# Five reorderings at the ends of three stages, and the decay product one slot earlier, in a two-block fp32 kernel on one core

## The chip, the cores and the metric

The kernel runs on one NeuronCore of a Trainium2 chip, in one launch. The metric is the device time of one execution in microseconds (us). The five engines are named as in the profile: PE is TensorE, DVE is VectorE, ACT is ScalarE, POOL is GpSimd, SP is SyncE. They run their own instruction streams in order and meet only at semaphores.

## The reference

One sequence of 512 tokens, 1024 channels, passes two layers of a first block and one layer of a second. The first layer is a state-space mixer (SSD): a normed input is projected, convolved and gated, and 32 heads in 8 groups run a chunked scan in both directions. Cut to its core, per chunk of 128 tokens:

```python
cum = jnp.cumsum(lac, axis=1)
decay = jnp.exp(jnp.where(causal, cum[:, :, None] - cum[:, None], -jnp.inf))
cb = jnp.einsum('blgn,bsgn->blsg', cc, bc)
y = jnp.einsum('blsgr,bsgrp->blgrp', cb[..., None] * decay, xdt)
y = y + jnp.einsum('blgn,bgrpn->blgrp', cc, state) * jnp.exp(cum)[..., None]
```

The two directions and a skip term are added, the sum is gated by silu(z), normed within its group and multiplied by an output matrix into the residual. The second layer is gated linear attention (GLA) with the same outer form. The second block projects its normed input for a convolution branch and a latent attention with rotary positions, merges them, adds a cross attention and an MLP. All is float32.

## The kernel before, in words

Every large product is streamed. A unit is a 128-row weight block of up to 1024 columns; SP loads it (`load_unit`, line 119), ACT rounds it to its high part (`split_hi`, line 129, instruction on line 137), DVE subtracts to get the low part (`split_lo`, line 140, instruction on line 147), and PE multiplies it in three products per 128 channels (`mm3`, lines 79 to 81) inside `stream_products` (line 159). That function waits for the low part and for a free one of three PSUM banks, and skips a unit that was already streamed (`if n < c.streamed: return`, with a counter kept while the program is built). SP may load unit n only when unit n-2 is split, so a late `split_lo` is a late load; other loads of SP stand in the same queue.

The SSD stage (`ssd_stage`, line 317) is written out by hand as rounds i = 0 to 9 of 8 slots k. In round i, the units of group i are projected (slots 2 and 3: x; 5 and 6: B and C), while the scan of group g = i-1 is computed and the gate z and the norm of earlier groups are finished. From round 3 on, slots 4 and 7 hold the products with the output matrix (`SSD_OUT`, line 288); in rounds 1 and 2 slots 4 and 7 have no unit at all, in round 8 slots 3, 4, 6 and 7. "Round (i, k)" below is round i, slot k. Each engine walks the same slots. What matters here:

- ACT, per slot: the centre tap of the convolution of the unit before (line 870), z (882), `split_hi`, exponentials (895), copies of x (902), the decay's differences for the next groups (929, 935), which wait for rows that SP loads (line 648), and in slot 7 silu of x, B, C and z between two table loads (940 to 947).
- POOL builds cb times dt for four token tiles (lines 736, 740), adds differences (713), and finishes y (703, 707).
- DVE, per slot: the other four taps of the convolution (line 995), `close` for output tiles (adds a PSUM bank to the residual h and frees it, line 963), `split_lo`, the masked cb (1043), x times decay weights (1054), in slots 2 to 5 the decay matrix m(0) to m(3) (line 1073, two buffers), the states (1082, 1087, 1090), and `assemble(g, p)` (977, 980), which turns the sums of head pair p into y: pair 0 as the last thing in slot 7, pair 1 in slot 0 of the next round, behind that slot's `split_lo`.
- PE, per slot: the unit's product; in slot 0 transposes of x and B and the product of B and C (lines 831, 834, 839), which wait for the silu and for both `assemble` of the group before (`s_asm`, 6 g); `contributions` to the states in slots 2 to 4 (773); `y_intra(g, t)` (757), the product of m(t) and x, in slots 3 to 6, after that slot's unit; `y_inter` (788) in slot 6 three times, six products each, and once in slot 7, where it reuses a PSUM bank that `assemble(g, 0)` must have read:

```python
if (p, d) == (1, 1):
    pe.wait_ge(s_asm, 6 * g + 2)
```

In the last rounds of SSD and GLA, `scale_tile` (ACT, line 243) writes the high part of the next stage's input, `scale_rest` (DVE, line 249) its low part, `square_tile` (ACT, 203 and 205) its squares, of which GLA needs two kinds per tile, and `add_squares` (POOL, 217 and 220) sums them; PE multiplies the sums by ones (258; after GLA 1327 and 1328, behind DVE's line 1609).

`mix_project_stage` (line 1691) has 14 units in slots k = 0 to 13. In slot 6 DVE splits unit 8, then multiplies the unit of the rotary key by a sine (lines 1856 to 1866); PE waits in slot 7 for that (line 1763), behind unit 7. In slot 7 DVE refines a norm (lines 184 to 190, 1848), subtracts (1853) and copies the bank of unit 6 (1876).

Of the kernel before, what the change touches and what calls it, by code (L numbers as in the profile page):

```python
# [27 lines left out]
SG = 8  # L28
# [288 lines left out]
def ssd_stage(nc, c, A, plan, gain):  # L317
# [8 lines left out]
    with ExitStack() as ctx:  # L326
# [421 lines left out]
        def _(pe):  # L748
# [42 lines left out]
            for i, k in slots:  # L791
# [27 lines left out]
                if g not in G:  # L819
                    continue  # L820
                if k == 0:
                    pe.wait_ge(s_silu, g + 1)
                    if g == 0:
                        pe.wait_ge(s_v, 17)
                        pe.wait_ge(s_a, 5)
                    if g:
                        pe.wait_ge(s_asm, 6 * g)
                    for t in range(NT):
                        for j in range(2):
                            a = (t % 2) * GW + j * P  # L830
                            pe.transpose(q[t // 2][:, a:a + P], xt[:, g % 2, j, t * P:(t + 1) * P],
                                         c.ident[:, :])
                    for t in range(NT):
                        last = pe.transpose(q[2][:, t * P:(t + 1) * P], bct[:, 0, t * P:(t + 1) * P],
                                            c.ident[:, :])
                    last.then_inc(s_tx, 1)
                    for t in range(NT):
                        b = slice(t * P, (t + 1) * P)
                        last = pe.matmul(q[3][:, b], bct[:, 0, b], cmat(g)[:, b], start=True, stop=True)
                    last.then_inc(s_cb, 1)  # L840
                if 2 <= k <= 4:
                    contributions(g, k - 2)
                if 3 <= k <= 6:
                    y_intra(g, k - 3)
                if k == 6:
                    for d in range(2):
                        y_inter(g, 0, d)
# [103 lines left out]
        def _(dve):  # L951
# [32 lines left out]
            for i, k in slots:  # L984
                g, f = i - 1, i - 2
                pi, pk = before(i, k)
                if pi in G and pk in CONV:
                    cj = CONV[pk]
                    t, ct = tile_of(pi, pk), conv_tile(pi, cj)
                    dve.wait_ge(s_center, 4 * pi + cj + 1)  # L990
                    dst, src = conv_out(pi, cj), bank(c, t)
                    for tp, last in ((0, 0), (1, 0), (3, 0), (4, 1)):
                        o = tp - 2
                        a, b = max(0, -o), T - max(0, o)
                        ins = dve.scalar_tensor_tensor(out=dst[:, a:b], in0=src[:, a + o:b + o],  # L995
                                                       scalar=tap(tp, ct), in1=dst[:, a:b], op0=ALU.mult,
                                                       op1=ALU.add)
                        if last:
                            ins.then_inc(c.bank_free[t % SB], 1)
                        else:  # L1000
                            ins.then_inc(s_tap, 1)
                            taps[0] += 1
                            dve.wait_ge(s_tap, taps[0])
# [12 lines left out]
                if (pi, pk) in SSD_OUT:  # L1016
                    of, half = SSD_OUT[pi, pk]
                    for j in range(1, 4):
                        close(pi, pk, j)
                        if of == SG - 1:  # L1020
                            scale_rest(c, dve, nx, half * 4 + j - 1)
                    if of == SG - 1:
                        scale_rest(c, dve, nx, half * 4 + 3)
                if (i, k) == (NI - 1, 0):
                    assemble(f, 1)
                if unit_in(i, k) is not None:
# [49 lines left out]
                if 3 <= k <= 5 and g in G:  # L1076
# [6 lines left out]
                    else:  # L1083
                        dve.wait_ge(s_st, 7 * g + 3 * j - 2)
                        for d, t in ((0, j), (1, NT - 1 - j)):
# [3 lines left out]
                        dve.wait_ge(s_st, 7 * g + 3 * j)  # L1089
                        dve.tensor_tensor(st[:, j, :], st[:, j, :], q[2 + j % 2][:, :], ALU.add)\  # L1090
                           .then_inc(s_st, 1)
                if k == 7 and g in G:
                    assemble(g, 0)
            next_fine(c, dve, nx)

# [34 lines left out]
def gla_stage(nc, c, A, plan, gain, gains):  # L1130
# [10 lines left out]
    with ExitStack() as ctx:  # L1141
# [190 lines left out]
        def _(act):  # L1332
# [15 lines left out]
            for i, k in slots:  # L1348
# [4 lines left out]
                if GLA_OUT.get((pi, pk), (0,))[0] == GH - 1:  # L1353
                    _, m0, tiles = GLA_OUT[pi, pk]
                    for m in range(m0, m0 + tiles):
                        final = free_value(c, out_tile(GH - 1, m))
                        scale_tile(c, act, nx, m, final)
                        square_tile(c, act, m, final)
                        square_tile(c, act, m, final, gain)
                if k == 0 and f in G:  # L1360
# [330 lines left out]
def mix_project_stage(nc, c, A, cqh, cql, ckh, ckl, tbl, ks, z):  # L1691
# [3 lines left out]
    with ExitStack() as pre:  # L1695
# [107 lines left out]
        def _(dve):  # L1803
# [4 lines left out]
            for k in range(N + 1):  # L1808
                t = tile(k - 1) if k else None
                if 1 <= k <= 5:  # L1810
                    dve.wait_ge(c.tile_done, t + 1)
                    dve.tensor_tensor(lat[:, k - 1, :], bank(c, t)[:, :], c.rstd, ALU.mult)\
                       .then_inc(c.bank_free[t % SB], 1)
                if k < N:
                    split_lo(c, dve, n0 + k + 2)
                if k == 1:
# [25 lines left out]
                if k in (5, 7):  # L1842
# [3 lines left out]
                    for j in (range(3), range(3, 5))[e]:  # L1846
# [5 lines left out]
                    lo, hi, src = ((cql, cqh, lat[:, 0:3, :]), (ckl, ckh, lat[:, 3:5, :]))[e]  # L1852
                    dve.tensor_tensor(lo[:, :, :], src, hi[:, :, :].bitcast(F32), ALU.subtract)\
                       .then_inc(s_ll, 1)
                if k == 6:
                    dve.wait_ge(s_ta, 1)
                    dve.tensor_scalar(tbl[:, :], tbl[:, :], cst[:, 2:3], None, ALU.mult).then_inc(s_tb, 1)
                    dve.wait_ge(s_tb, 12)
                    dve.wait_ge(c.tile_done, t + 1)
                    dve.tensor_tensor(krt[:, :], bank(c, t)[:, :], tbl[:, :], ALU.mult)\  # L1860
                       .then_inc(c.bank_free[t % SB], 1)
                    dve.wait_ge(*free_value(c, t))
                    dve.tensor_tensor(krt[:, :], krt[:, :], c.rstd, ALU.mult).then_inc(s_tb, 1)

                    dve.tensor_scalar(tbl[:, :], tbl[:, :], float(QN + QR) ** -0.5, None, ALU.mult)\
                       .then_inc(s_tb, 1)
                if k == 8:
                    dve.wait_ge(s_kh, 1)
                    dve.tensor_copy(ks[64:P, 1, :], q[2][64:P, :]).then_inc(s_kl, 1)
# [1207 lines left out]
```

## Time and profile before

| what | us |
|---|---|
| median of the runs (lowest, highest) | 1791.13 (1789.34, 1793.04) |
| profiled execution, own time | 1790.72 |
| span of the profiled execution | 1789.0 |
| PE busy in the span | 1688.9 |
| DVE, ACT, POOL busy | 1127.9, 841.1, 367.2 |
| mean granted TensorE clock | 0.981 of full speed |

The span is what the trace covers, from the first to the last instruction; the own time is that of the same execution as the runs measure it. In the page, busy times are shares of that span. The clock line of the page is 9 in its first slices, 8 in the second to fourth of the 40, and 9 in nearly all others.

### The profile page before, as it was taken

What the parts mean: (1) busy time and instruction counts of PE and PEld (TensorE: products, weight loads), DVE (VectorE), ACT (ScalarE), POOL (GpSimd) and SP (SyncE); (2) the same over time, 40 slices, a digit from 0 to 9 for tenths busy, and PEclk for the clock granted to TensorE, in tenths of its full rate; (3) what the DMA queues carried; (4) which work ended last, traced back from release to release, by engine and by line L of the source; (5) the groups of instructions that cost most, each with busy time, mean ns of one, the idle gap of its engine ahead of it and who ended that gap; (6) DMA issues with size and microseconds to landing.
All of it is one profiled execution on the core that took longest, in us unless ns stands there. A gap on an engine that the chain in (4) does not pass through costs nothing.

```text
span 1789.0 us, 20987 instructions
## 1 busy us (share of the span) xinstructions
PE 1688.9 (94%) x7944; PEld 1359.6 (76%) x7944; DVE 1127.9 (63%) x1520; ACT 841.1 (47%) x1365; POOL 367.2 (21%) x299
## 2 busy tenths in 40 slices
PE   6888999999989999999988899999899899999998
PEld 4766778777767788787866678887688688888886
DVE  6677777887777575756567767776556553434343
ACT  5656656656624354435354434447354442323232
POOL 0354554445531000000006112230220200000001
PEclk9889999999999999999999999999999999999999
DMA  3633444344312222222222232232233233333332
GB/s 106 182 113 112 131 126 133 118 142 124 89 44 81 57 71 71 78 76 71 60 83 65 71 80 67 60 81 92 74 91 103 86 95 95 95 96 104 95 95 71
DMA packets 260107, 164.58 MB, mean 92 GB/s; under 512 B 26910, under 2 KB 249287, under 8 KB 258983
## 3 DMA queue, kind: packets, MB, share of 16 engines
q1 hardware_dynamic: 260006, 163.25, 31.8%
q8 instruction: 63, 1.03, 0.2%
q14 instruction: 38, 0.30, 0.1%
HBM read 160.86 MB, written 2.36 MB: 91 GB/s over the span
## 4 chain that ended last, share of the span: by engine, by line
PE 71%; DVE 14%; ACT 6%; issue 4%; POOL 2%; DMA 2%; SPq 0%; DVEq 0%; ACTq 0%; POOLq 0%
PE stream L79 20%; PE stream L81 19%; PE stream L80 19%; DVE weights_lo L147 2%; DVE ssd_x L995 2%; ACT weights_hi L137 1%; PE q L1977 1%; PE q L2001 1%; PE q L79 1%; PE q L788 1%; PE q L81 1%; PE q L80 1%; POOL h_sum_of_squares L220 1%; DVE ssd_m L1073 1%; PE q L817 1%
## 5 line engine op out<-in xcount | busy, mean ns | idle before, releaser
L79 PE MATMUL stream<-u_lo,weights_hi 128*128 128x512 f32 (+2 forms) x1312 | 532.7, 406 | 11.7 <-DVE u_lo L249 4.5
L81 PE MATMUL stream<-u_hi,weights_hi 128*128 128x512 f32 (+2 forms) x1312 | 515.7, 393 | 0.0
L80 PE MATMUL stream<-u_hi,weights_lo 128*128 128x512 f32 (+2 forms) x1312 | 515.4, 393 | 0.0
L147 DVE TENSOR_TENSOR weights_lo<-weights_raw,weights_hi 128x1024 fp32r<-128x1024 f32 (+4 forms) x269 | 330.4, 1229 | 281.0 <-ACT weights_hi L137 280.8
L137 ACT ACTIVATE weights_hi<-weights_raw 128x1024 fp32r<-128x1024 f32 (+4 forms) x269 | 268.6, 1000 | 458.4 <-PE stream L81 431.2
L79 PEld LDWEIGHTS stream<-u_lo,weights_hi 128*128 128x128 f32 (+2 forms) x1312 | 248.7, 190 | 77.8 <-issue 9.7
L80 PEld LDWEIGHTS stream<-u_hi,weights_lo 128*128 128x128 f32 (+2 forms) x1312 | 248.3, 189 | 54.8 <-issue 4.9
L81 PEld LDWEIGHTS stream<-u_hi,weights_hi 128*128 128x128 f32 (+2 forms) x1312 | 247.5, 189 | 55.3 <-issue 0.5
L217 POOL COPY h_sum_of_squares<-h_squares 128x512 f32<-128x512 f32 x5 | 3.2, 649 | 790.9 <-ACT h_squares L205 790.9
L79 PE MATMUL stream<-mlp_a_lo,weights_hi 128*128 128x512 f32 x256 | 100.2, 391 | 0.0
L81 PE MATMUL stream<-mlp_a_hi,weights_hi 128*128 128x512 f32 x256 | 99.7, 389 | 0.0
L80 PE MATMUL stream<-mlp_a_hi,weights_lo 128*128 128x512 f32 x256 | 99.6, 389 | 0.0
L713 POOL TENSOR_TENSOR ssd_cum_steps<-ssd_cum_steps 128x512 f32<-128x512 f32 x32 | 57.2, 1787 | 161.4 <-ACT ssd_cum_steps L929 161.2
L929 ACT ACTIVATE ssd_cum_steps<-ssd_cum_steps,ssd_cum_at_cols 128x128 f32<-128x128 f32 x256 | 77.8, 390 | 10.8 <-DMA ssd_cum_steps<-ssd_cum_rows 10.8
L736 POOL TENSOR_TENSOR ssd_work<-ssd_cb,ssd_dt_cols 128x512 f32<-128x512 f32 x64 | 67.2, 1071 | 36.6 <-DVE ssd_m L1073 19.7
L2852 DVE SCALAR_TENSOR_TENSOR mlp_relu<-stream,h_squares 128x512 f32<-128x512 f32 x32 | 22.1, 691 | 70.2 <-PE stream L81 70.1
L1946 POOL TENSOR_TENSOR mix_conv<-mix_conv,att_tap_products 128x512 f32<-128x512 f32 x30 | 40.3, 1342 | 121.8 <-ACT att_tap_products L2060 119.8
L220 POOL TENSOR_TENSOR h_sum_of_squares<-h_sum_of_squares,h_squares 128x512 f32<-128x512 f32 x34 | 49.4, 1452 | 72.2 <-ACT h_squares L205 70.3
L995 DVE SCALAR_TENSOR_TENSOR ssd_bc<-stream,params,ssd_bc 128x510 f32<-128x510 f32 (+1 forms) x64 | 47.9, 749 | 24.8 <-ACT ssd_bc L870 23.1
L2129 DVE SCALAR_TENSOR_TENSOR q<-mix_z,params,q 128x512 f32<-128x512 f32 x76 | 57.0, 750 | 1.7
L995 DVE SCALAR_TENSOR_TENSOR ssd_x<-stream,params,ssd_x 128x510 f32<-128x510 f32 (+1 forms) x64 | 47.8, 748 | 12.5 <-ACT ssd_x L870 10.6
L81 PEld LDWEIGHTS stream<-mlp_a_hi,weights_hi 128*128 128x128 f32 x256 | 48.1, 188 | 10.0
(468 smaller groups left out, 2891.1 us busy)
## 6 DMA issues: line engine op xcount, KB each, us to landing
weights_raw<-in_w_mlp_dram SPq DMA_DIRECT2D x64, 512.0 KB, 3.8
weights_raw<-in_ssd_w_in_dram SPq DMA_DIRECT2D x48, 512.0 KB, 4.1
weights_raw<-in_gla_w_in_dram SPq DMA_DIRECT2D x40, 512.0 KB, 3.8
ssd_cum_steps<-ssd_cum_rows SPq DMA_DIRECT2D x32, 512.0 KB, 5.0
weights_raw<-in_w_in_dram SPq DMA_DIRECT2D x29, 512.0 KB, 3.8
ssd_exp_cum<-ssd_cum_pairs SPq DMA_DIRECT2D x16, 512.0 KB, 7.6
weights_raw<-in_ssd_w_out_dram SPq DMA_DIRECT2D x16, 512.0 KB, 3.6
weights_raw<-in_gla_w_out_dram SPq DMA_DIRECT2D x13, 512.0 KB, 3.4
```

The source lines that it names most:

```text
L79: pe.matmul(out, lh, rl, start=first, stop=False, skip_group_check=skip)
L80: pe.matmul(out, ll, rh, start=False, stop=False, skip_group_check=skip)
L81: return pe.matmul(out, lh, rh, start=False, stop=last, skip_group_check=skip)
L137: act.activation(w_view(c, n)[0], raw_view(c, n), ACT.Copy).then_inc(c.w_rounded, 1)
L147: dve.tensor_tensor(lo, raw_view(c, n), hi.bitcast(F32), ALU.subtract).then_inc(c.w_split, 1)
L220: pool.tensor_tensor(acc[:, :], acc[:, :], c.sq[:, n % 2, :], ALU.add).then_inc(c.square_added, 1)
L713: pool.tensor_tensor(flat_steps[0], flat_steps[0], flat_steps[1], ALU.add).then_inc(s_join, 1)
L736: pool.tensor_tensor(ways[d].rearrange("p (h l) -> p h l", h=HPG), again(cbm[:, d, t * P:(t + 1) * P], HPG), spread(head(dtc, d, t, g), P) ...
L929: last = act.activation(steps[:, r, d, h, :], steps[:, r, d, h, :], ACT.Relu, scale=-1.0, bias=at_cols[:, t, col:col + 1])
L995: ins = dve.scalar_tensor_tensor(out=dst[:, a:b], in0=src[:, a + o:b + o], scalar=tap(tp, ct), in1=dst[:, a:b], op0=ALU.mult, op1=ALU.add)
L1946: pool.tensor_tensor(acc[:, LAST, :], acc[:, LAST, :], prod[:, e % 2, :], ALU.add)\
L2129: dve.scalar_tensor_tensor(out=dst, in0=src, scalar=par[:, w:w + 1], in1=q[4][:, :], op0=ALU.mult, op1=ALU.add).then_inc(s_tap, 1)
```

## The change

It touches six places. On PE, the product of unit (1, 1) is issued in slot (1, 0), before the wait for the first silu. On PE, `y_intra` moves to slots 2 to 5, for all groups. On DVE, where slot 7 has no output unit (rounds 1, 2 and 8), `assemble(g, 0)` becomes the first thing of the slot. On DVE, in the last group of SSD, all `close` of a unit come before the four `scale_rest`. On ACT, in the last group of GLA, both `scale_tile` come before the squares. On DVE, in slot 6 of the projection, the rotary key comes before `split_lo` of unit 8 and behind nothing of that slot.

```diff
@@ ssd_stage, PE
                 if k == 0:
+                    if g == 0:
+                        stream_products(c, pe, unit_in(1, 1), lambda j: c.uh[:, j, :], lambda j: c.ul[:, j, :])
                     pe.wait_ge(s_silu, g + 1)
@@
                 if 2 <= k <= 4:
                     contributions(g, k - 2)
-                if 3 <= k <= 6:
-                    y_intra(g, k - 3)
+                if 2 <= k <= 5:
+                    y_intra(g, k - 2)
@@ ssd_stage, DVE
                 pi, pk = before(i, k)
+                alone = k == 7 and g in G and (i, k) not in SSD_OUT
+                if alone:
+                    assemble(g, 0)
                 if pi in G and pk in CONV:
@@
                     for j in range(1, 4):
                         close(pi, pk, j)
-                        if of == SG - 1:
-                            scale_rest(c, dve, nx, half * 4 + j - 1)
                     if of == SG - 1:
-                        scale_rest(c, dve, nx, half * 4 + 3)
+                        for j in range(4):
+                            scale_rest(c, dve, nx, half * 4 + j)
@@
-                if k == 7 and g in G:
+                if k == 7 and g in G and not alone:
                     assemble(g, 0)
@@ gla_stage, ACT
                     for m in range(m0, m0 + tiles):
+                        scale_tile(c, act, nx, m, free_value(c, out_tile(GH - 1, m)))
+                    for m in range(m0, m0 + tiles):
                         final = free_value(c, out_tile(GH - 1, m))
-                        scale_tile(c, act, nx, m, final)
                         square_tile(c, act, m, final)
                         square_tile(c, act, m, final, gain)
@@ mix_project_stage, DVE (the block stood after the block of k in (5, 7))
+                if k == 6:
+                    dve.wait_ge(s_ta, 1)
+                    dve.tensor_scalar(tbl[:, :], tbl[:, :], cst[:, 2:3], None, ALU.mult).then_inc(s_tb, 1)
+                    dve.wait_ge(s_tb, 12)
+                    dve.wait_ge(c.tile_done, t + 1)
+                    dve.tensor_tensor(krt[:, :], bank(c, t)[:, :], tbl[:, :], ALU.mult)\
+                       .then_inc(c.bank_free[t % SB], 1)
+                    dve.wait_ge(*free_value(c, t))
+                    dve.tensor_tensor(krt[:, :], krt[:, :], c.rstd, ALU.mult).then_inc(s_tb, 1)
+
+                    dve.tensor_scalar(tbl[:, :], tbl[:, :], float(QN + QR) ** -0.5, None, ALU.mult)\
+                       .then_inc(s_tb, 1)
                 if k < N:
                     split_lo(c, dve, n0 + k + 2)
```

## Rows read from the trace of the kernel before

**Rows 1.** The page, first part: busy time of PE and its weight load.

```profile
PE 1688.9 (94%) x7944; PEld 1359.6 (76%) x7944; DVE 1127.9 (63%) x1520; ACT 841.1 (47%) x1365; POOL 367.2 (21%) x299
```

**Rows 2.** PE's waits over the span: sum in us, times, longest.

```profile
PE q L788 <- DVE ssd_state_parts L980: 12.7, 3, 7.0
...
PE q L831 <- ACT ssd_bc L942: 5.3, 1, 5.3
...
PE q L1763 <- DVE mixp_key_rope L1863: 4.2, 1, 4.2
PE stream L79 <- DVE ssd_x L995: 4.1, 5, 0.8
```

**Rows 3.** Timeline of SSD round 1, slots 0 to 4: start, duration, instruction, [idle before].

```profile
69.97 1.97 PE L831 MATMUL q<-ident,ssd_x 128*128 128x128 f32 x8 [5.32 <-ACT ssd_bc L942]
...
76.86 0.58 ACT L882 ACTIVATE ssd_z<-stream 128x512 f32<-128x512 f32 x1
...
85.22 1.51 DVE L1073 TENSOR_TENSOR ssd_m<-ssd_work,ssd_cum_steps 128x512 f32<-128x512 f32 x1 [1.18 <-POOL ssd_work L740]
...
86.52 0.58 PE L79 MATMUL stream<-u_lo,weights_hi 128*128 128x512 f32 x1
...
92.20 1.02 PE L773 MATMUL q<-ssd_xw,ssd_b_tok 128*128 128x256 f32 x4
...
96.23 1.23 DVE L1073 TENSOR_TENSOR ssd_m<-ssd_work,ssd_cum_steps 128x512 f32<-128x512 f32 x1
```

**Rows 4.** Timeline of SSD round 1, slot 6, to round 2, slot 0.

```profile
107.97 2.27 PE L788 MATMUL q<-ssd_bc,ssd_state 128*128 128x128 f32 x18
...
109.35 2.44 ACT L929 ACTIVATE ssd_cum_steps<-ssd_cum_steps,ssd_cum_at_cols 128x128 f32<-128x128 f32 x8 [6.42 <-DMA ssd_cum_steps<-ssd_cum_rows]
...
113.01 3.10 DVE L995 SCALAR_TENSOR_TENSOR ssd_bc<-stream,params,ssd_bc 128x510 f32<-128x510 f32 x4 [3.74 <-ACT ssd_bc L870]
...
117.28 1.65 PE L788 MATMUL q<-ssd_bc,ssd_state 128*128 128x128 f32 x6 [7.04 <-DVE ssd_state_parts L980]
...
124.66 1.02 DVE L980 TENSOR_TENSOR ssd_state_parts<-q,ssd_exp_cum 128x384 f32<-128x384 f32 x2
...
126.39 1.03 PE L831 MATMUL q<-ident,ssd_x 128*128 128x128 f32 x8
```

**Rows 5.** Timeline of SSD round 2, slot 4, to round 3, slot 0.

```profile
152.85 0.68 DVE L1073 TENSOR_TENSOR ssd_m<-ssd_work,ssd_cum_steps 128x512 f32<-128x512 f32 x1
...
167.16 3.10 DVE L995 SCALAR_TENSOR_TENSOR ssd_bc<-stream,params,ssd_bc 128x510 f32<-128x510 f32 x4 [2.78 <-ACT ssd_bc L870]
...
171.44 1.65 PE L788 MATMUL q<-ssd_bc,ssd_state 128*128 128x128 f32 x6 [5.00 <-DVE ssd_state_parts L980]
...
179.98 1.06 PE L831 MATMUL q<-ident,ssd_x 128*128 128x128 f32 x8 [0.67 <-DVE ssd_state_parts L980]
```

**Rows 6.** Timeline of SSD round 5, slot 3; rounds 3 to 7 repeat it.

```profile
316.77 1.76 DVE L1073 TENSOR_TENSOR ssd_m<-ssd_work,ssd_cum_steps 128x512 f32<-128x512 f32 x1
...
317.79 0.66 PE L757 MATMUL q<-ssd_m,ssd_x_pair 128*64 128x128 f32 x8
```

**Rows 7.** Timeline of SSD round 8, slot 4, on PE.

```profile
488.69 2.07 PE L773 MATMUL q<-ssd_xw,ssd_b_tok 128*128 128x256 f32 x4 [2.42 <-DVE ssd_state L1082]
```

**Rows 8.** Timeline of SSD round 9, slots 4 to 7, on DVE and PE.

```profile
529.69 2.77 DVE L249 SCALAR_TENSOR_TENSOR u_lo<-h,params,u_hi 128x512 fp32r<-128x512 f32 x2
...
535.33 0.50 PE L79 MATMUL stream<-ssd_y_lo,weights_hi 128*128 128x512 f32 x1 [2.21 <-DVE h L963]
```

**Rows 9.** Timeline of the end of GLA, on ACT, POOL and PE.

```profile
944.71 0.72 ACT L243 ACTIVATE u_hi<-h,first_and_mix_gains 128x512 fp32r<-128x512 f32 x1 [0.57 <-DVE h L1492]
...
946.03 1.34 POOL L220 TENSOR_TENSOR h_sum_of_squares<-h_sum_of_squares,h_squares 128x512 f32<-128x512 f32 x1 [0.80 <-ACT h_squares L205]
...
966.82 1.22 PE L1327 MATMUL q<-h_sum_of_squares,ones 128*128 128x512 f32 x1 [3.72 <-DVE gla_k L1609]
```

**Rows 10.** Timeline of the projection's slots 6 and 7 on DVE.

```profile
1015.87 1.23 DVE L147 TENSOR_TENSOR weights_lo<-weights_raw,weights_hi 128x1024 fp32r<-128x1024 f32 x1 [2.55 <-ACT weights_hi L137]
...
1020.34 0.68 DVE L184 TENSOR_SCALAR mixp_turns<-q 128x512 f32<-128x512 f32 x1
```

More of the change, by code:

```diff
@@ L1854, in _ @@
                        .then_inc(s_ll, 1)
[L1855 to L1866, printed above, removed]
                 if k == 8:
```

## The prediction

> **What bounds it.** I read the page first, then the list of PE's waits, then the timeline around each wait. The page gives PE 94% busy [rows 1], so only gaps and half-speed stretches can be won. Of the waits [rows 2], the change aims at three: 12.7 us of `y_inter` in slot 7 (7.04 in round 1, 5.00 in round 2, the rest in round 8), 5.3 us before the first transposes and 4.2 us before the rotary key. The question for each is what is late next. My sum is made against the profiled execution's own time, 1790.72, which is 0.4 under the median of the runs, 1791.13; a measurement of this kernel can tell 0.2%, 3.6 us, from no change.
>
> **Unit (1, 1) early.** PE fills the 5.32 us. But what PE needs in slot 2 doesn't move: ACT reaches its copy of z only at 76.86 [rows 3], long after that tile was done, since it works through silu, table load and differences without a pause. Behind it stand `split_hi`, DVE's mask, POOL's products and m(0), which starts at 85.22. Alone the edit would let product (1, 3) start some us before its 86.52. With `y_intra(0, 0)` now ahead of it, it starts after m(0): 85.22 + 1.51 + 0.66 = 87.4. The whole lead is gone, 0.9 us and more.
>
> **`y_intra` early, rounds 1 and 2.** Slot 4 has no unit there, and `y_intra(g, 2)` now stands in it and needs m(2), which DVE makes in that slot behind the convolution of unit (i, 3). I follow round 1 with PE at full speed. A product takes 92.20 - 86.52 = 5.7 [rows 3]; (1, 3) ends at 93.1; ACT's centre tap takes 0.8, the taps 3.1 (as the four in [rows 4]), m(2) 0.7, so 97.8. `y_intra` 0.7, products (1, 5) and (1, 6) with `y_intra(0, 3)` between, 5.7 + 0.6 + 5.7, bring PE to 110.5; the first 12 of `y_inter` take 12/18 of 2.27 less the tail, 1.3 [rows 4], so 111.8.
>
> **`assemble` first in slot 7.** It starts there and takes 0.74 + 0.91, so DVE is free at 113.4. Only then comes the convolution of C, which started at 113.01 [rows 4]: +0.4. PE's slot 7 loses its wait, yes. But the transposes of round 2 wait for the second `assemble`, and its path runs from that convolution through silu, table load, `split_hi` and `split_lo`: from 113.01 to 124.66 + 1.02 = 125.7. PE came at 126.39, 0.7 later. So no more than 0.7 us can be won in round 1, whatever the 7.04 were; they become a wait of some 6 us in front of the transposes. In round 2 nothing can be won: PE already waited there, at 179.98 [rows 5]. By the same steps, m(2) ends at 153.53; plus 0.7 + 5.7 + 0.6 + 5.7 + 1.3 + 1.65 the convolution of C starts at 169.1 in place of 167.16: +1.9, all passed on.
>
> **Half speed.** After the waits before rows 69.97, 117.28, 171.44 and 488.69 PE ran at half clock: eight transposes took 1.97 after the wait, 1.03 without [rows 3, 4]; six of `y_inter` 1.65; four contributions 2.07 against 1.02 at 92.20 [rows 3, 7]. A short stretch cost about 1.5 us (488.69: 1.05, and the next eight small ones 0.46), the one at 69.97 about 2.9 (0.94 + 0.46 + 0.7 in slot 0, 0.8 in the product behind). The new waits: in round 1 before m(0) (about 6 us in two parts, near sure) and before m(2) (2.9 us), in round 2 before m(2) (2.9 us); the trace has waits of 2 to 3 us mostly with such a stretch behind them, so I give the short ones 0.8. They delay the convolution of C by 1.5 x 1.8 = 2.7 and 1.5 x 0.8 = 1.2. The waits of 6 us before the transposes of rounds 2 and 3 fall on the path in full: 1.5 to 2.9, I take 2.3. The Trainium skill ("TensorE: Matmul & The Clock Gate", Part 4: PE-mode transpose) says that transposes don't count as busy like other matmuls; by it the upper end, 2.9, would be right and the sum 1.2 higher.
>
> Round 1: +0.4 + 2.7 - 0.7 + 2.3 = +4.7 (bounds: 0.4 - 0.7 + 1.5 = +1.2, and 0.4 + 3.0 - 0.7 + 2.9 = +5.6). Round 2: +1.9 + 1.2 + 2.3 = +5.4 (bounds +3.4 and 1.9 + 1.5 + 2.9 = +6.3).
>
> **Rounds 3 to 7.** m(0) is there in slot 2. In slot 3 PE is 0.6 later by `y_intra(0)` and then needs m(1), done at 316.77 + 1.76 = 318.5, about when the old `y_intra(0)` ended (317.79 + 0.59 = 318.4) [rows 6]. Slot 4's product starts 0.8 later, and meets its bank wait of 0.8 for the taps, five times in the span [rows 2], which takes it up. Slot 6 has no `y_intra` any more: -0.6 a round. The next transposes keep 0.1 of slack to the second `assemble`. I take 5 x 0.55 = -2.8 (bounds -3.0 and 0). Round 8: m(1) replaces the wait for the state [rows 7]: -0.4 (-0.5 and 0); `assemble` first changes nothing there, for nothing stood before it.
>
> **`close` before `scale_rest`.** In round 9 DVE follows PE's tiles; the first two `scale_rest` (0.74 each) ran while it waited for tiles 2 and 3. Moved behind, they delay `split_lo` and the `close` for which PE waits at 535.33 [rows 8] by 2 x 0.75 = 1.5, and at most by 2 x 1.39 if both run as slowly as the pair at 529.69 (beside POOL). POOL has no more work than before, so the lower price is nearer; +0.1 for the second half: +1.6 (+1.5 and +2.8). The Trainium skill ("SBUF — State Buffer", "SBUF: two separate sides") calls the port pair of the two engines an exclusive lock for a whole instruction; by it the number of POOL's instructions sets the delay, and the sum stays.
>
> **Scale before squares.** PE gets its last input 1 us sooner, but then waits for the sums at 966.82 [rows 9]. POOL adds back to back from 946.03, where it had waited 0.80 for ACT's square; that square now stands behind a second scale, 0.7 [rows 9]. +0.6 (0 and +0.8).
>
> **Rotary key first.** The key's steps need the sine, done at about 1013.5, and no weights. The wait of 4.17 shrinks to 0.6; then PE waits for unit 8's split, which ends at 1015.87 + 1.23 = 1017.1 as before [rows 10]: the product that began at 1020.09 can begin at 1017.15, -2.9. Two products on, PE needs the bank that DVE frees behind the refinement, 1020.34 [rows 10], which moves by 2.0 only (the norm's rough value is there at 1018.0). Taken: -2.0 (-2.9, and -0.5 if half speed follows the new waits).
>
> **Sum.** 4.7 + 5.4 - 2.8 - 0.4 + 1.6 + 0.6 - 2.0 = +7.1, 1797.8 against the own time, 1798.2 against the median. Lowest ends together: 1.2 + 3.4 - 3.0 - 0.5 + 1.5 + 0 - 2.9 = -0.3; highest 5.6 + 6.3 + 2.8 + 0.8 - 0.5 = +15.0.
>
> **Rivals.** (a) The waits are too short to drop the clock, except before the transposes: 7.1 - 2.7 - 1.2 - 1.6 for transposes at the short price = +1.6, 1792.7. For it: the later waits of the trace don't all lose speed. Against: four of four named rows do. 0.21. (b) The steady rounds give nothing: m(1) is made beside POOL, and if POOL's work falls later it takes longer than 1.76; with the long price for the transposes, 7.1 + 2.8 + 1.2 = +11.1, 1802. 0.12. (c) Faster: the chain before the second `assemble` isn't what holds the transposes. If the convolution of C could start before 113.01 and 167.16, the waits would really go: -7.0 - 5.0 for slot 7, half of them kept since `assemble` stays ahead, and -2.8 - 2.0 besides: about -9, 1782. Its place is the start of that convolution; it decides from 2 us earlier on. Against it: DVE waited there for ACT, and ACT for rows whose load began only after a `split_lo` (the 6.42 at 109.35 [rows 4]), which nothing in the change moves forward. 0.05. My own case has 0.62, and holds +3.7 to +10. That the change doesn't do what it says I leave out: order and the skip are fixed when the program is built.
>
> **How the numbers follow.** Slower by over 0.2% (above 1794.7): 0.62 + 0.12 = 0.74; within 0.2%: 0.21; faster: 0.05. The range leaves out most of (c), and the ends of (a) and (b): 1792 to 1803.
>
> **What would show it.** Right: no wait on line 788 in rounds 1 and 2, but one of 5 to 7 us on line 831 for line 980 in each; waits of about 3 us on line 757 for line 1073 in slot 4 of those rounds; the convolution of C later by 2 to 4 us; rounds of 57.2 in place of 57.8 later on; line 1763's wait under 1. Wrong: transposes of round 2 starting at or before 126, or a period that stays.

## The result: 0.46% slower, and the profile after

The median of the changed kernel is 1799.79 us (four runs, 1796.55 to 1800.69) against 1790.56 for the kernel before (1789.34 to 1793.04). The ratio is 1.0046, with a 95% interval of 1.0030 to 1.0061: +8.2 us. The profiled execution took 1796.55, the fastest of the four; its span is 1794.8, 5.8 more than before.

The page of the changed kernel, busy times: PE is no busier than in [rows 1]. What was lost is idle time.

```profile
PE 1687.6 (94%) x7944; PEld 1356.3 (76%) x7944; DVE 1114.6 (62%) x1520; ACT 841.1 (47%) x1365; POOL 368.2 (21%) x299
```

PE's waits after the change: sum in us, times, longest. They answer to [rows 2].

```profile
PE q L833 <- DVE ssd_state_parts L982: 13.4, 2, 6.7
...
PE q L757 <- DVE ssd_m L1077: 8.5, 4, 3.6
...
PE q L1331 <- DVE gla_k L1614: 5.1, 1, 5.1
...
PE q L773 <- DVE ssd_xw L1058: 3.6, 1, 3.6
...
PE stream L79 <- DVE mixp_linear L1881: 2.6, 1, 2.6
...
PE q L788 <- DVE ssd_state_parts L982: 2.1, 3, 0.7
...
PE q L1768 <- DVE mixp_key_rope L1827: 0.7, 1, 0.7
```

Lines have moved by 2 to 5: L833 are the transposes (831 before), L1077 is m(t), L982 and L979 are `assemble`, L1000 is the convolution. The 12.7 us of `y_inter` became 2.1, and 13.4 stand in front of the transposes. 8.5 us on the decay matrix and 3.6 on x times weights are new.

Timeline of the changed kernel, PE in SSD round 1, slots 2 to 4 (start, duration, instruction, [idle before]); it answers to [rows 3].

```profile
81.76 2.08 PE L773 MATMUL q<-ssd_xw,ssd_b_tok 128*128 128x256 f32 x4 [3.58 <-DVE ssd_xw L1058]
...
85.64 1.12 PE L757 MATMUL q<-ssd_m,ssd_x_pair 128*64 128x128 f32 x8 [1.80 <-DVE ssd_m L1077]
86.68 0.80 PE L79 MATMUL stream<-u_lo,weights_hi 128*128 128x512 f32 x1
...
94.51 1.02 PE L773 MATMUL q<-ssd_xw,ssd_b_tok 128*128 128x256 f32 x4
...
99.28 0.66 PE L757 MATMUL q<-ssd_m,ssd_x_pair 128*64 128x128 f32 x8 [2.10 <-DVE ssd_m L1077]
```

The early unit brings PE to slot 2 some 4 us sooner, and there it waits twice, for things that did not move. Product (1, 3) starts at 86.68 in place of 86.52 and lasts to 94.51: 7.8 us, in place of 5.7, because it begins at half speed.

DVE and PE from slot 7 of round 1 to slot 0 of round 2, one list for each engine; they answer to [rows 4].

```profile
113.32 0.75 DVE L979 SCALAR_TENSOR_TENSOR ssd_y<-ssd_x,params,q 128x512 f32<-128x512 f32 x1 [2.64 <-issue]
113.99 1.01 DVE L982 TENSOR_TENSOR ssd_state_parts<-q,ssd_exp_cum 128x384 f32<-128x384 f32 x2
114.92 1.52 DVE L1000 SCALAR_TENSOR_TENSOR ssd_bc<-stream,params,ssd_bc 128x510 f32<-128x510 f32 x2
...
114.59 0.94 PE L788 MATMUL q<-ssd_bc,ssd_state 128*128 128x128 f32 x6 [0.69 <-DVE ssd_state_parts L982]
...
127.72 1.94 PE L833 MATMUL q<-ident,ssd_x 128*128 128x128 f32 x8 [6.71 <-DVE ssd_state_parts L982]
...
131.87 0.72 PE L79 MATMUL stream<-u_lo,weights_hi 128*128 128x512 f32 x1
```

`assemble` runs first, `y_inter` hardly waits, and the transposes come 1.33 us later than before (126.39), after a wait of 6.71. The product of unit (2, 1) then starts 4.15 us behind them; before it was 2.12 (from 126.39 to 128.51, where 24 matmuls of the stream begin).

The clock behind that: PE in the 4.3 us of this stretch, and in the 2.1 us of the same instructions before (stretch; its length; busy time of PE, PEld, DVE, ACT, POOL with instructions; granted clock; DMA share; GB/s).

```profile
127.70:132.00 4.30, 4.28 (x21) 4.30 (x21) 1.56 (x1) 1.45 (x4) 3.54 (x3) 0.50 0.70 198
```

```profile
126.40:128.50 2.10, 2.10 (x21) 2.10 (x20) 0.34 (x1) 1.92 (x3) 1.97 (x2) 1.00 0.50 150
```

The same 21 instructions take twice the time: 1.2 GHz in place of 2.4, after a wait of 6.71 and after none.

Round 2 in the changed kernel, DVE, POOL and PE; it answers to [rows 5].

```profile
156.48 1.78 DVE L1077 TENSOR_TENSOR ssd_m<-ssd_work,ssd_cum_steps 128x512 f32<-128x512 f32 x1
...
175.56 0.74 DVE L1000 SCALAR_TENSOR_TENSOR ssd_bc<-stream,params,ssd_bc 128x510 f32<-128x510 f32 x1
...
156.44 1.27 POOL L713 TENSOR_TENSOR ssd_cum_steps<-ssd_cum_steps 128x512 f32<-128x512 f32 x1
...
158.31 0.66 PE L757 MATMUL q<-ssd_m,ssd_x_pair 128*64 128x128 f32 x8 [3.57 <-DVE ssd_m L1077]
...
188.36 1.94 PE L833 MATMUL q<-ident,ssd_x 128*128 128x128 f32 x8 [6.72 <-DVE ssd_state_parts L982]
192.52 0.77 PE L79 MATMUL stream<-u_lo,weights_hi 128*128 128x512 f32 x1
```

The convolution of C starts at 175.56 in place of 167.16, the transposes of round 3 at 188.36 in place of 179.98.

**Where the time went.** I count every trace from its own first product with 128 rows (27.03 before, 25.98 after), which leaves out the start. "Gates, GLA" is the first product of GLA's gates (551.13 before), "memory rows" the first transposes of the memory's rows (1315.10 before). In us against the trace before:

| kernel | transposes, round 2 | product (2, 1) | transposes, round 3 | product (3, 1) | product (8, 1) | gates, GLA | memory rows, near 1315 |
|---|---|---|---|---|---|---|---|
| changed | +2.4 | +4.4 | +9.4 | +11.4 | +9.4 | +9.0 | +6.8 |

Round 1 costs 4.4, round 2 7.0, rounds 3 to 7 give back 2.1. Rounds 8 and 9 give 0.4, in which +1.8 for `close` first is contained. Of the rest, 2.5 came back inside GLA, between its gates and its last products, where no instruction differs: the kernel before ran three stretches there at half speed (rows of 0.63 from 553.73, 625.30 and 932.41) and the changed one none. That part is no gain of the change.

### The profile page after: what moved, and what is told of

Same layout as the page of the kernel before. It is cut to its first block, busy times and chain, and to the rows that moved or that the text cites. A ratio compares the mean times of both kernels' runs of the same rounds, so it can differ in the third digit from the quotient of the medians.

```text
span 1794.8 us, 20987 instructions
## 1 busy us (share of the span) xinstructions
PE 1687.6 (94%) x7944; PEld 1356.3 (76%) x7944; DVE 1114.6 (62%) x1520; ACT 841.1 (47%) x1365; POOL 368.2 (21%) x299
## 3 DMA queue, kind: packets, MB, share of 16 engines
q8 instruction: 63, 1.03, 0.2%
## 4 chain that ended last, share of the span: by engine, by line
PE 69%; DVE 15%; ACT 7%; issue 5%; POOL 2%; DMA 1%; SPq 0%; DVEq 0%; ACTq 0%; POOLq 0%
PE stream L79 19%; PE stream L81 19%; PE stream L80 19%; DVE weights_lo L147 2%; ACT weights_hi L137 2%; DVE ssd_x L1000 2%; PE q L1982 1%; PE q L2006 1%; PE q L79 1%; DVE ssd_m L1077 1%; PE q L81 1%; PE q L80 1%; PE q L817 1%; PE q L788 1%; ACT gla_contribution L1371 1%
## 5 line engine op out<-in xcount | busy, mean ns | idle before, releaser
L147 DVE TENSOR_TENSOR weights_lo<-weights_raw,weights_hi 128x1024 fp32r<-128x1024 f32 (+4 forms) x269 | 321.0, 1195 | 282.2 <-ACT weights_hi L137 281.8
L713 POOL TENSOR_TENSOR ssd_cum_steps<-ssd_cum_steps 128x512 f32<-128x512 f32 x32 | 53.6, 1674 | 170.1 <-ACT ssd_cum_steps L931 170.1
L1000 DVE SCALAR_TENSOR_TENSOR ssd_bc<-stream,params,ssd_bc 128x510 f32<-128x510 f32 (+1 forms) x64 | 47.9, 749 | 23.2 <-ACT ssd_bc L872 21.5
L1000 DVE SCALAR_TENSOR_TENSOR ssd_x<-stream,params,ssd_x 128x510 f32<-128x510 f32 (+1 forms) x64 | 47.8, 748 | 19.5 <-ACT ssd_x L872 17.8
```

The source lines that it names most:

```text
L147: dve.tensor_tensor(lo, raw_view(c, n), hi.bitcast(F32), ALU.subtract).then_inc(c.w_split, 1)
L713: pool.tensor_tensor(flat_steps[0], flat_steps[0], flat_steps[1], ALU.add).then_inc(s_join, 1)
```

## Experiments

All ratios are to the kernel before, timed beside each kernel on the same chip; the us are the ratio times 1791. An unedited round is one that the edits of a run don't touch. The table at the end of this section has their traces, counted as above.

**Single edits.**

```diff
 # e1: unit (1, 1) alone
                 if k == 0:
+                    if g == 0:
+                        stream_products(c, pe, unit_in(1, 1), lambda j: c.uh[:, j, :], lambda j: c.ul[:, j, :])
 # e2: y_intra alone
-                if 3 <= k <= 6:
-                    y_intra(g, k - 3)
+                if 2 <= k <= 5:
+                    y_intra(g, k - 2)
 # e3: assemble(g, 0) first in slot 7 of rounds 1, 2 and 8, alone
+                alone = k == 7 and g in G and (i, k) not in SSD_OUT
+                if alone:
+                    assemble(g, 0)
```

> The kernel before with unit (1, 1) early as its only edit. Theory (round 1 is bounded by its start, and y_intra(0) took the lead away in the full change): without y_intra ahead of it, product (1, 3) starts 1.5 to 3 us before its 86.52, the transposes of round 1 run at full clock, but the convolution of C in slot 7 still waits for ACT, so about 0 to 2 us are kept: 1789 to 1791, ratio 0.999 to 1.000. Rival (the early unit itself delays round 1, by its bank or its loads): slower by 1 to 2 us.

Measured: 0.9997 (0.9989 to 1.0006), -0.5 us. The transposes of round 1 ran at full clock, product (1, 3) began at 83.49, and nothing was left of it in the times.

> The kernel before with y_intra in slots 2 to 5 as its only edit. Theory: waits for m(0) and m(2) in rounds 1 and 2 cost about 1.7 and 3.9 us on the chain through the convolution of C; rounds 3 to 7 give 2 to 3, round 8 gives 2; sum about +1.5 (0 to +3), 1792.5. Waits of 7 and 5 us in slot 7 stay, transposes run at full clock. Rival (y_intra early carries the loss of the whole change): +7 or more, 1798.

Measured: 0.9992 (0.9981 to 1.0002), -1.4 us, below the 0 to +3 of the theory: the loss in rounds 1 and 2 came (product (3, 1) is 5.4 later than in an unedited kernel), and the later rounds gave back more than was said. The rival falls: `y_intra` early doesn't carry the loss.

> The kernel before with assemble first in slot 7 as its only edit. Theory: the convolution of C keeps its start within 0.5 us in both rounds, because assemble fits into DVE's wait of 3.7 and 2.8 us; the waits of 7.0 and 5.0 us on PE move in front of the transposes, which then run at half clock, 1.9 in place of 1.0 each, with half speed behind them: +1.5 in round 1 and +2.5 in round 2, +4 in all (+2 to +6), 1795. Rival (c of the prediction: the waits really go): -9, 1782. Second rival (moved waits cost nothing): 0.

Measured: 1.0032 (1.0020 to 1.0045), +5.7 us. This edit alone, meant to remove 12 us of waiting, is the loss. Both rivals fall. Its trace, DVE and then PE in rounds 1 and 2:

```profile
109.75 0.75 DVE L977 SCALAR_TENSOR_TENSOR ssd_y<-ssd_x,params,q 128x512 f32<-128x512 f32 x1 [0.40 <-issue]
...
112.91 3.10 DVE L998 SCALAR_TENSOR_TENSOR ssd_bc<-stream,params,ssd_bc 128x510 f32<-128x510 f32 x4 [1.48 <-ACT ssd_bc L870]
...
168.27 3.10 DVE L998 SCALAR_TENSOR_TENSOR ssd_bc<-stream,params,ssd_bc 128x510 f32<-128x510 f32 x4
...
111.02 0.94 PE L788 MATMUL q<-ssd_bc,ssd_state 128*128 128x128 f32 x6 [0.69 <-DVE ssd_state_parts L980]
```

In round 1 `assemble` fits into DVE's wait, as expected: the convolution of C still waits 1.48 for ACT, `y_inter` starts 6.3 us sooner than in [rows 4], and the transposes come no sooner than in an unedited round, after 8.27 of waiting (-1.4 in the table below, where e4 and e5 have -1.5 and -1.6). Product (2, 1) stands at +0.1 where e4 and e5 stand at -1.5 and -1.6, product (3, 1) at +2.4 against -1.6. So the trace shows +4.0 for rounds 1 and 2; the rest of the 5.7 lies within the interval. Nearly all of the 4.0 is half speed behind the two moved waits: about 1.7 between the transposes of round 2 and product (2, 1), passed on to the transposes of round 3, and about 2.0 behind those.

**The changed kernel with that edit taken back** (`assemble(g, 0)` last in slot 7 again).

> The changed kernel with assemble(g, 0) put back behind the rest of slot 7. Theory: of round 1's +4.4 and round 2's +7.0 about 3 us each go, since the transposes of rounds 2 and 3 run at full clock again and the convolution of C needs no assemble ahead of it: 1794 against the 1799.8 of the changed kernel (ratio to before 1.001 to 1.003). Rival (the loss is all in y_intra early): the time stays within 1 us of 1799.8.

Measured: 1.0016 (1.0007 to 1.0024), +2.9 us, in place of the +8.2 of the whole change. The two ways of pricing the edit agree: 5.7 alone, 5.3 within the whole. The transposes took 1.03 and began without a wait.

**The two PE edits together**, nothing else.

> The kernel before with unit (1, 1) early and y_intra in slots 2 to 5 for all groups, nothing else. The sum of the single edits is -0.5 - 1.4 = -1.9. Theory: with both, PE comes early to two waits in a row in round 1 slot 2 (3.6 for contributions, 1.8 for m(0)) and the product behind them runs at half clock, which neither edit alone shows: the transposes of round 2 come 1 to 2 us later than before, and the time is +1 to +2. Rival (the edits add, and the missing 3 us of the whole change lie elsewhere): -2.

Measured: 0.9999 (0.9990 to 1.0007), -0.2 us: neither. The trace does show the two losses adding up to more than their parts: the transposes of round 2 stand at +1.4, where each edit alone stands at -1.5 and -1.3 and an unedited round at -1.6. So in this one trace they cost 3 us in round 1 that neither costs alone, by these waits (PE, round 1, slot 2, in the run with both):

```profile
83.28 1.49 PE L773 MATMUL q<-ssd_xw,ssd_b_tok 128*128 128x256 f32 x4 [3.56 <-DVE ssd_xw L1056]
...
87.15 1.12 PE L757 MATMUL q<-ssd_m,ssd_x_pair 128*64 128x128 f32 x8 [2.38 <-DVE ssd_m L1075]
88.20 0.80 PE L79 MATMUL stream<-u_lo,weights_hi 128*128 128x512 f32 x1
```

But the time doesn't show it: against the -1.9 of the sum of the single edits, -0.2 is within the intervals. That stays open.

**The three edits at the ends of stages** (`close` first, scale first, key first).

> The kernel before with the last three edits only: close before scale_rest at the end of SSD, scale before squares at the end of GLA, rotary key first. In the trace of the changed kernel they moved PE by +1.8, about -0.5 and about -0.9. Theory: they are worth what that trace shows, +0.5 in all (-1 to +2), ratio 1.000. Rival (the difference between the single edits and the whole, 8.2 measured less 5.7, -1.4 and -0.5, is theirs): +4, ratio 1.002.

Measured: 1.0007 (0.9998 to 1.0016), +1.3 us, between the two and nearer to the theory. The sum -0.5 - 1.4 + 5.7 + 1.3 = +5.1 lies just under the whole's interval (5.4 to 10.9); with the two PE edits as timed together (-0.2 in place of -1.9) it is +6.8, inside it. The 3 us that the trace shows for the pair would make it +8, but no timing bears them out.

**`y_intra` early where nothing is late.**

```diff
+                late = 2 if g >= 2 else 3
+                if late <= k <= late + 3:
+                    y_intra(g, k - late)
```

> The kernel before with y_intra in slots 2 to 5 for groups 2 to 7 only; groups 0 and 1 keep slots 3 to 6. Theory: no new waits in rounds 1 and 2, and rounds 3 to 7 at 57.2 to 57.3 in place of 57.8 each: -2.1 to -2.8, with round 8 -2 more: -4 to -5, 1787.5 to 1788.5, ratio 0.9975. Rival (the gain of a steady round is taken back in round 9 or GLA by half-speed stretches that fall elsewhere): within 1 us of the kernel before.

Measured: 0.9969 (0.9959 to 0.9979), -5.6 us. Taking the edit out of two groups turned -1.4 into -5.6. Rounds 3 to 7 gave 2.7 (from -1.5 to -4.2 in the table), and rounds 8 and 9 2.2 more, of which some is chance: e1, which edits nothing there, gained 1.2.

**The place that the prediction named as the one that decides.** Rival (c) said that `assemble` first would pay only if the convolution of C could start earlier, and that ACT held it. So ACT's centre tap of C goes ahead of the differences that wait for rows:

```diff
             for i, k in slots:
                 ...
                     act.activation(conv_out(pi, cj), bank(c, t)[:, :], ACT.Identity, scale=tap(2, ct),
                                    bias=par[:, at["ssd_conv_b"] + ct:at["ssd_conv_b"] + ct + 1])\
                        .then_inc(s_center, 1)
+                if k == 7 and i in (1, 2):
+                    differences(i, 6)
                 ...
+                if k != 6 or i not in (1, 2):
+                    differences(i, k)
```

`differences` holds the two loops over `CUT` and `DECAY`, unchanged.

> The kernel before, but in rounds 1 and 2 ACT makes the centre tap of C (first thing of its slot 7) ahead of slot 6's differences and exponential, which wait for rows that SP loads. assemble stays last. Theory: the start of the convolution of C is what holds the chain to the transposes; it moves from 113.01 to 109.5 and from 167.16 to 164.5, slot 7's wait on PE shrinks by as much, and the transposes of rounds 2 and 3 start 3 us earlier each (less what they wait then for other things): -4 to -6, 1786. Rival (another chain, through the second assemble or the unit's split in slot 0, holds the transposes): under 1 us gained.

Measured: 0.9962 (0.9949 to 0.9974), -6.8 us, a little more than the theory's 4 to 6. Its trace, ACT, DVE and PE at the end of round 1 and PE in round 3:

```profile
107.21 0.78 ACT L887 ACTIVATE ssd_bc<-stream,params 128x512 f32<-128x512 f32 x1 [4.56 <-PE stream L81]
109.12 2.45 ACT L865 ACTIVATE ssd_cum_steps<-ssd_cum_steps,ssd_cum_at_cols 128x128 f32<-128x128 f32 x8 [1.13 <-DMA ssd_cum_steps<-ssd_cum_rows]
...
108.92 3.10 DVE L1002 SCALAR_TENSOR_TENSOR ssd_bc<-stream,params,ssd_bc 128x510 f32<-128x510 f32 x4
...
113.20 1.65 PE L788 MATMUL q<-ssd_bc,ssd_state 128*128 128x128 f32 x6 [3.23 <-DVE ssd_state_parts L987]
121.73 1.07 PE L831 MATMUL q<-ident,ssd_x 128*128 128x128 f32 x8 [0.58 <-DVE ssd_state_parts L987]
...
172.70 1.07 PE L831 MATMUL q<-ident,ssd_x 128*128 128x128 f32 x8 [0.50 <-DVE ssd_state_parts L987]
```

The tap is made while the rows are still on their way; the convolution starts at 108.92 (113.01 in [rows 4]) and the transposes at 121.73 (126.39). Start for start the chain passes its gain on.

**The same with `assemble` first.**

> The same with assemble(g, 0) first in slot 7 as well. Theory: the convolution of C must now wait for assemble, which waits for y_inter, so it starts at about 112 in place of 109.5; the transposes wait about 5 us and run at half clock: 3 to 6 us slower than the run with the centre tap alone, 1790 to 1792. Rival (the price of assemble first came only from the late centre tap): as fast as the run with the centre tap alone, or faster.

Measured: 1.0020 (1.0011 to 1.0029), +3.6 us: 10.4 slower than with the tap alone, far more than the 3 to 6 of the theory. DVE and PE at the end of round 1:

```profile
108.52 0.75 DVE L984 SCALAR_TENSOR_TENSOR ssd_y<-ssd_x,params,q 128x512 f32<-128x512 f32 x1 [0.41 <-issue]
...
110.11 3.09 DVE L1005 SCALAR_TENSOR_TENSOR ssd_bc<-stream,params,ssd_bc 128x510 f32<-128x510 f32 x4
...
122.91 1.94 PE L831 MATMUL q<-ident,ssd_x 128*128 128x128 f32 x8 [6.73 <-DVE ssd_state_parts L987]
```

The convolution starts 1.19 later than with the tap alone and the transposes 1.18 later; then half speed takes 1.9 (4.08 us to product (2, 1) against 2.15). In round 2 the same happens again, with DVE held until PE's `y_inter` is through. Product (3, 1) is 7.3 later for it. Most of the rest comes in GLA, where no instruction differs.

**The edits that gained, together.**

> The two edits that gained, together: the centre tap of C first in rounds 1 and 2 (measured 0.9962) and y_intra in slots 2 to 5 for groups 2 to 7 (0.9969). Theory: they act in different rounds and add: -6.8 - 5.5 = -12.3, 1779, ratio 0.993. Rival (part of each was the same luck with half-speed stretches in round 8 and GLA): -8 to -9, 0.995.

Measured: 0.9956 (0.9944 to 0.9968), -7.9 us: the rival. In the times they don't add. Up to GLA they can: e14 below, which has the same instructions as this run until the projection, stands at -12.6 at the gates, and loses 3.4 from there to the memory rows.

> The same with the rotary key ahead of the split. Theory: the wait of 4.2 before the key goes, one of 2.6 on a bank and a colder product take most of it; -0.9 as in the trace of the changed kernel, -1 against the run without it. Rival (the prediction's term): -2.

Measured: 0.9944 (0.9929 to 0.9960), -10.0 us; median 1783.42, lowest 1776.27. Against the run without the key the intervals overlap.

> The same with unit (1, 1) early as well. Theory: alone it was worth 1.5 us at the transposes of round 2 and its y_intra(0) stays in slot 3 here, so it keeps 0 to 1.5 us. Rival (it loses speed in the wait before contributions, which lasts 3.6 us, and gives nothing): 0 to +1.

Measured: 0.9952 (0.9936 to 0.9969), -8.6 us. It adds nothing that can be seen.

Any of the last three is faster than both kernels; which is best isn't settled by these runs. All traces, in us against the trace before, from their own first product:

| kernel | transposes, round 2 | product (2, 1) | transposes, round 3 | product (3, 1) | product (8, 1) | gates, GLA | memory rows |
|---|---|---|---|---|---|---|---|
| e1 unit (1, 1) early | -1.5 | -1.5 | -1.8 | -1.9 | -1.9 | -3.1 | -0.1 |
| e2 `y_intra` early | -1.3 | -1.3 | +2.1 | +3.8 | +1.1 | -2.7 | -2.7 |
| e3 `assemble` first | -1.4 | +0.1 | +0.4 | +2.4 | +3.1 | +5.5 | +7.4 |
| e4 `y_intra` early, groups 2 to 7 | -1.5 | -1.5 | -1.5 | -1.5 | -4.2 | -6.4 | -3.5 |
| e5 stage ends | -1.6 | -1.6 | -1.7 | -1.7 | -1.7 | -1.1 | +0.5 |
| e8 changed, `assemble` last | +1.4 | +1.4 | +5.8 | +5.8 | +3.1 | +3.0 | +4.9 |
| e16 both PE edits | +1.4 | +1.4 | +5.7 | +5.7 | +3.0 | +1.0 | +1.0 |
| e11 tap first | -4.4 | -4.4 | -7.0 | -7.0 | -6.9 | -6.8 | -6.8 |
| e12 tap and `assemble` first | -3.3 | -1.4 | -1.1 | +0.3 | +0.2 | +0.3 | +3.1 |
| e13 tap, groups 2 to 7 | -5.3 | -5.3 | -7.9 | -6.3 | -9.0 | -8.5 | -6.6 |
| e14 with key first | -5.1 | -5.1 | -7.7 | -7.7 | -10.4 | -12.6 | -9.3 |
| e15 with unit early | -5.0 | -5.0 | -7.6 | -7.6 | -10.3 | -12.5 | -9.1 |

e4 and e5 don't touch round 1 and stand at -1.5 and -1.6 there: the trace before was itself slow by as much in that round, so +4.4 for the changed kernel's round 1 is nearer to +6 against an ordinary execution.

## Why the prediction was right, and where it was not

The forecast was 1798.2 and slower, for one reason above the others: the 12 us of waiting in slot 7 were no slack, since the transposes hang on a chain that starts at the convolution of C. That was tested from both sides. Removing the wait without moving the chain cost 5.7 us; moving the chain (by 4.1 us in round 1) without removing the wait gained 6.8. The signs that were named came: no wait over 0.7 on `y_inter`, 6.71 and 6.72 before the transposes, 2.10 and 3.57 before m(2), a period of 57.25, 0.7 before the rotary key. The convolution of C came 3.0 later in round 1 and 5.0 more in round 2, where 2 to 4 was said.

- **`assemble` first.** "They become a wait of some 6 us in front of the transposes": 6.71 and 6.72. Half speed behind them, taken as 2.3 each: 2.03 and 2.01 to the next product. Right.
- **Unit (1, 1) early.** "The whole lead is gone": product (1, 3) at 86.68 where 87.4 was said; this execution was 1.05 ahead from the start. Right, but the half speed behind m(0) was taken as 1.5, and it was 2.6: `y_intra` 1.12 for 0.66, the product 7.8 for 5.7. That the contributions took 2.08 for 1.02 cost nothing, for they were done before the wait of 1.80 for m(0).
- **Round 1: +4.7, measured +4.4.** The convolution of C moved by +3.0 (114.92 against 113.01, and 1.05 for the earlier start), where 3.1 was said. That came out by cancelling: the half speed behind m(0) was 1.1 more than its 1.5, and the m(2) wait, with 1.2 set down for it, had none behind it. Part of the +4.4 is luck too: against an unedited round it is nearer to +6, over the upper bound of 5.6.
- **Round 2: +5.4, measured +7.0, above the upper bound of 6.3.** The step that failed is "m(2) ends at 153.53": it priced m(2) at the 0.68 of [rows 5], and in the changed kernel it took 1.78, +1.1. In all 14 traces POOL's addition and m(2) start within 0.04 us of each other in this slot, and one of the two takes its short time and the other the long one. In the four kernels with `y_intra` early for all groups it was m(2) that took long; in the other ten it was m(2) four times, and kernels with the same instructions up to there differ. So luck and the change aren't told apart here. The kernel before, then e5, whose SSD rounds 1 to 8 are those of the kernel before:

```profile
152.83 1.85 POOL L713 TENSOR_TENSOR ssd_cum_steps<-ssd_cum_steps 128x512 f32<-128x512 f32 x1
152.85 0.68 DVE L1073 TENSOR_TENSOR ssd_m<-ssd_work,ssd_cum_steps 128x512 f32<-128x512 f32 x1
```

```profile
151.58 1.30 POOL L713 TENSOR_TENSOR ssd_cum_steps<-ssd_cum_steps 128x512 f32<-128x512 f32 x1
151.59 1.84 DVE L1072 TENSOR_TENSOR ssd_m<-ssd_work,ssd_cum_steps 128x512 f32<-128x512 f32 x1
```

  The term should have been 0.68 or 1.8, with a chance for each. It counts only because `y_intra(2)` now waits for m(2) there. The half-speed stretch behind that wait, taken at 0.8 of 1.5, came in full: product (2, 5) lasted 7.3 in place of 5.7. The Trainium skill ("SBUF — State Buffer", "SBUF: two separate sides") has the two engines exclude each other for a whole instruction; the traces agree: in the changed kernel m(2) ends 0.55 after the addition that started 0.04 before it, which is nearly its own 0.68, and in the kernel before the addition ends 1.15 after m(2), which is nearly its own 1.27.
- **Rounds 3 to 7: -2.8, measured -2.1.** The period was right: 57.25 in place of 57.78, from the transposes of rounds 4 and 8. Round 3 gave nothing, because its first product ran partly at half speed behind the moved wait.
- **Rounds 8 and 9: -0.4 + 1.6, measured -0.4 in all.** `close` first cost what was said: the wait for it grew by 1.0 and one of 0.8 for the low part was added. Round 8 gave 1.9 in place of 0.4: the step that failed costed the loss of the 2.42 wait, not that of the half speed behind it, though [rows 7] showed that too. That half speed doesn't always come. In e1, whose round 8 is unedited, the same wait has none behind it (1.13 where [rows 7] has 2.07), so two traces don't tell how much of the 1.9 the edit gives by itself:

```profile
486.28 1.13 PE L773 MATMUL q<-ssd_xw,ssd_b_tok 128*128 128x256 f32 x4 [2.40 <-DVE ssd_state L1084]
```

- **Scale first: +0.6, measured +1.0 at the norm's sums and +1.4 behind them, above its bound of 0.8.** PE's last products of GLA started 5.4 later than before, the product of the norm's sums 6.48 later (973.30 against 966.82), and just before the rotary key PE was 6.8 behind, all in the traces' own times.
- **Key first: -2.0, measured -0.8.** Before it the changed kernel was 6.8 behind, after it 6.0. The product that "can begin" 2.9 sooner did (1023.98 against 1020.09), and by its end PE stood only 1.6 behind, since it ran at full speed where the one before had not. But DVE's copy of the bank stood at 1031.56 against 1026.92, 2.2 sooner, as said, and the product that needs the bank started 2.5 sooner (1032.38 against 1028.06). Then this followed (PE, the projection's slot 8, changed kernel):

```profile
1032.38 0.47 PE L79 MATMUL stream<-u_lo,weights_hi 128*128 128x512 f32 x1 [2.63 <-DVE mixp_linear L1881]
...
1033.66 0.63 PE L81 MATMUL stream<-u_hi,weights_hi 128*128 128x512 f32 x1
```

A new wait of 2.63, then matmuls of 0.63 where they took 0.39: 1.7 back. Half speed behind the new wait was a bound of the term (-0.5) and should have been its value.

**The sum.** It was +7.1, the times say +8.2, and the profiled execution +6.8 at the memory rows. The last of these agrees partly by luck: the parts above come to 4.4 + 7.0 - 2.1 - 0.4 + 1.4 - 0.8 = +9.5, and the 2.5 that GLA gave back without an edit bring it down again.

**The rivals.** (a), short waits that don't drop the clock, is half true: behind m(2)'s 2.10 in round 1 there was no half speed, behind its 3.57 in round 2 there was, and behind the 2.4 of round 8 there was in the kernel before and not in e1. (b), steady rounds that give nothing, fell. (c) fell as a forecast and held as a mechanism: the start of the convolution decides. It was wrong in one point. It supposed that the tap early and `assemble` first would gain together; with the tap early, `assemble` first costs 10.4 us, because it ties DVE to PE's `y_inter`.

## What to carry to other kernels

A wait on the busiest engine is worth only what the next wait behind it allows: before removing it, follow the chain of the instruction that waits next, and look for the engine that stands in front of that chain with something that isn't due. Here a few instructions of ACT, put behind the one that was due, gained 6.8 us, where the six edits of the change lost 8.2. An edit that is good in the steady rounds should be left out of the first ones, where the same slot is short of its input.

## What the runs showed that was not expected

A wait can cost more than its length, and a faster product before it can make it dearer. e13 and e14 have the same instructions up to the projection. Product (3, 0), just before the transposes of round 3, ran at full speed in e13 and partly at half speed in e14, so PE was there sooner in e13. The transposes in e13, then in e14:

```profile
172.88 1.94 PE L831 MATMUL q<-ident,ssd_x 128*128 128x128 f32 x8 [2.14 <-DVE ssd_state_parts L988]
```

```profile
173.68 1.06 PE L831 MATMUL q<-ident,ssd_x 128*128 128x128 f32 x8 [0.51 <-DVE ssd_state_parts L988]
```

The transposes begin at the same time, counted from the first product (-7.9 and -7.7), but the faster execution waited 2.14 for them and lost the clock: at product (3, 1) it is 1.4 behind. By the gates of GLA, e14 is 4.1 us ahead of e13.

The same shows in GLA, where the instructions are the same in all these kernels, but for the order of scales and squares in the last group. Windows from 560 to 960 of the kernel before, the changed one and e4 (columns as above):

```profile
560.00:960.00 400.00, 384.08 (x1776) 312.87 (x1774) 251.65 (x350) 182.63 (x260) 17.48 (x13) 0.99 0.25 71
```

```profile
560.00:960.00 400.00, 384.26 (x1787) 312.58 (x1786) 250.87 (x353) 183.56 (x261) 11.90 (x9) 1.00 0.26 73
```

```profile
560.00:960.00 400.00, 384.92 (x1754) 312.65 (x1753) 247.34 (x338) 180.53 (x255) 18.72 (x13) 0.97 0.25 72
```

With a granted clock of 0.97 in place of 0.99, e4 lost 4.4 us against the kernel before in this window: it was 5.6 ahead at 560 and 1.2 ahead at 957. From the gates to the memory rows, e1, e4 and e12 lose 2.8 to 3.1 us that the kernel before and e11 don't, and in e3 one unit's product in the middle of GLA (741.06) took 8.3 us in place of 5.7. That is as large as most edits here, and why two traces can't price an edit of 2 us. The Trainium skill ("TensorE: Matmul & The Clock Gate", Part 1: The HAM clock gate) says that the monitor's window runs freely and that the number of slow matmuls therefore varies from run to run; these traces agree, with 4.1 us between e13 and e14 by the gates and 4.4 between e4 and the kernel before in GLA. Its Part 4 says that transposes don't count as busy like other matmuls. No run here separates that: behind the waits of 6.7 the clock was back within the next product of the changed kernel.
